# Where a two-layer decoder kernel computes the next layer's modulation: eight steps moved from the gate part to the output stage

## The chip, the cores and the metric

One Trainium2 chip, one core. The metric is the device time of one launch in microseconds, as the median of three runs. The engines are TensorE (PE, with its weight loads as PEld), VectorE (DVE), ScalarE (ACT), GpSimd (POOL) and SyncE (SP), which here only issues transfers.

## What is computed

Two layers over 256 tokens of 1024 channels. Each layer has a token mixer (retention and windowed attention) and a product-key retrieval over 128 x 128 single-neuron experts, and each is preceded by a normalization whose shift, scale and output gate depend on a condition vector:

```python
cond = jax.nn.silu(c)
for l in range(DEPTH):
    mod = cond @ ada_w[l] + ada_b[l]
    sh1, sc1, g1, sh2, sc2, g2 = jnp.split(mod, 6, axis=-1)
    h = rmsnorm(x, norm1_g[l]) * (1.0 + sc1[:, None]) + sh1[:, None]
    x = x + g1[:, None] * token_mixer(h, positions, w_in[l], ret_gn_g[l], sinks[l], w_out[l])
    h = rmsnorm(x, norm2_g[l]) * (1.0 + sc2[:, None]) + sh2[:, None]
    x = x + g2[:, None] * peer(h, peer_wq[l], peer_k1[l], peer_k2[l], peer_u[l], peer_v[l])
return rmsnorm(x, final_g)
```

`peer` picks 16 experts per head and token and computes `gelu(h . u[e]) * gate` for them, then the sum of these times `v[e]`. The kernel computes it densely for 224 of the 256 tokens: all `h . u` products, a matrix of gates that is zero for experts not picked, and all products with `v`. For the other 32 tokens it fetches the picked rows of `u` and `v`.

## The kernel before, in words

**Weight blocks.** All weights pass through the same pipeline in blocks of 128 x 1024 (512 KB). SP loads a block into one of four slots `raw` (L379), ScalarE rounds it into `w_hi` (`round_hi`, L552), VectorE makes the rest `w_lo = raw - w_hi` (`low`, L848), and TensorE multiplies with both. `w_hi` and `w_lo` have two slots each. A load waits until `low` of the block four earlier is done. Per layer there are 52 input blocks, 8 and 16 of two projections, 128 expert blocks `u` (numbered 0 to 127 here, the variable `m`) and 128 output blocks `v`. In the positions of the table below an output block has the number 128 (`N_U`) plus its own.

**The gate part.** The last 52 expert blocks, 76 to 127, run beside the building of the gate matrix in 28 batches of eight tokens. Batch b belongs to block `gate_after(b) = 76 + b * 50 // 28`: blocks 76, 77, 79, 81, 83, 84, 86, 88, 90, 92, 93, 95, 97, 99, 101, 102, 104, 106 and so on to 124, so that the distance is two blocks, and one block six times. In the block before its own, VectorE, ScalarE and GpSimd write the batch's one-hot operands (`hot`: on VectorE L1206 and L1210), then TensorE runs 16 small products behind the expert block (`gate`, L1703), which wait for all three. Beside them VectorE multiplies the activations with an earlier batch's gates (`weigh`, L1226, waits for the products of that batch) and with the next activation (`product`, L1233). TensorE's product of batch b also waits until batch b-2 is weighed.

**The output stage.** While TensorE works on output block m, ScalarE rounds a row block of the activations for block m+1 (`round_p`, L780) and VectorE makes its low rest (`low_p`, L1238) and the low rest of the weights (`low`). Then TensorE multiplies with `v`: first L1731, which begins only after `low_p`, then L1727, which waits for `low`. Beside this VectorE works for the 32 tokens: for 32 of the blocks 2 to 59 a dot product with a fetched row of `u` (`dot`, L1260, at block 2 + 57j//31), and for 32 of the blocks 61 to 118 a weighted addition of a fetched row of `v` (`mix`, L1277, at block 61 + 57j//31). GpSimd issues the fetch of the rows (L540).

**The modulation.** A modulation step is one `mod_block` (L852): VectorE multiplies a loaded block `ada` (128 x 1024) with the condition and sums along the row (L855). Every second one (odd number) also adds the bias to the last two sums (L859) and VectorE waits for that to be done. The steps are laid beside other work by tables of positions. `MOD_V_AT[l]` lists those of the expert and output blocks: `mod_beside(at)` is called once in each block, in the expert part right behind `low`, in the output stage behind `low_p` and `low` and ahead of `dot` and `mix`. SP loads step k's block (L391, two slots) right behind the weight block that stands five after the position of step k-2, if step k-2 is done. In layer 0 there are 18 such steps, numbers 46 to 63: the last two of layer 0's output gate, then shift and scale of layer 1's first normalization. In layer 1 there are two, at output blocks 4 and 10.

VectorE's order in an output block:

```python
if not (end and j == RING - 1):
    low_p(RING * i + j + 1, (j + 1) % 2)
if not (end and j == RING - 1 and l == DEPTH - 1):
    low(n0 + RING * i + j + 1, (j + 1) % RING)
mod_beside(N_U + RING * i + j)
for k in range(SP_STEPS):
    if dot_at(k) == RING * i + j:
        dot(k)
    if mix_at(k) == RING * i + j:
        mix(k)
```

Of the kernel before, what the change touches and what calls it, by code (L numbers as in the profile page):

```python
# [55 lines left out]
N_WOUT, N_WQ, N_U, N_V = KC, 2 * PH, NKEYS, NKEYS  # L56
# [16 lines left out]
          B_WQ + 1, B_WQ + 2, B_WQ + 3, B_WQ + 4, B_WQ + 5, B_WQ + 6)  # L73
PE_GROUP = 2
MOD_WIN = len(MOD_AT)
MOD_V_AT = (tuple(range(78, 78 + 3 * 16, 3)) + (N_U + 4, N_U + 10), (N_U + 4, N_U + 10))
MOD_L = (MOD_FIRST, MOD_FIRST + MOD_WIN + len(MOD_V_AT[0]))
assert MOD_L[1] + MOD_WIN + len(MOD_V_AT[1]) == DEPTH * N_MOD
V_COPIES = 5
# [143 lines left out]
def build(nc, x, c, positions, consts, decay, mask, vectors, ada, win, wout, wq, keys, u, v, u_rows, out):  # L223
    ctx = ExitStack()
    with ctx:
# [148 lines left out]
        def _(sp):  # L374
# [13 lines left out]
            def mod_load_v(n):  # L388

                sp.wait_ge(mod_used, n - 1)  # L390
                sp.dma_start(mod_ring2[:, n % 2, :], ada_all[n]).then_inc(mod_in2[n % 2], 16)  # L391
# [44 lines left out]
            for l in range(DEPTH):  # L436
                base = l * N_BLOCKS
                for q, (count, src) in enumerate(srcs):
# [39 lines left out]
                    def mods_beside(at):  # L478
                        for k in range(len(MOD_V_AT[l])):
                            if at == (MOD_V_AT[l][k - 2] + 5 if k > 1 else 4 * SPREAD_AT):  # L480
                                mod_load_v(MOD_L[l] + MOD_WIN + k)
# [358 lines left out]
        def _(dve):  # L840
# [119 lines left out]
            for l in range(DEPTH):  # L960
# [318 lines left out]
                def mod_beside(at):  # L1279

                    if at in MOD_V_AT[l]:
                        k = MOD_V_AT[l].index(at)
                        dve.wait_ge(mod_in2[k % 2], 16 * (len(MOD_V_AT[0]) // 2 * l + k // 2 + 1))
# [600 lines left out]
```

## Time and profile before

| | |
|---|---|
| three runs | 2009.29, 2010.58, 2012.95 us; median 2010.58 |
| profiled execution | 2010.33 us, its span from first to last instruction 2008.5 us |
| busy, share of the span | PE 97%, PEld 94%, DVE 85%, ACT 60%, POOL 22% |
| granted TensorE clock | 0.992 of full speed over the span |
| DMA | 480.55 MB, mean 239 GB/s |

The span is what the engines' timeline shows; the execution's own time is a little longer, by what lies around it. Shares are means over stages that have different limits, so the sections below read single stretches: the gate part of layer 0 is at about 515 to 686 us of the span, its output stage from 689 us on, and the same two stages of layer 1 start at about 1502 and 1671 us.

### The profile page before, as it was taken

Reading aid. Unit: us, or ns where it says so; the run is one execution under the profiler, and the core shown is the slowest. Engines: PE = TensorE matmul, PEld = TensorE weight load, DVE = VectorE, ACT = ScalarE, POOL = GpSimd, SP = SyncE. Lnnn points to the kernel's source line nnn. Section 1 sums busy time; section 2 is a strip of 40 time slices with the busy share of each in tenths; the row PEclk is TensorE's granted clock in tenths of the full one; section 3 lists DMA queues with packets and bytes.
Section 4 is the critical chain, followed back from the end, with each engine's and each line's share of the span. In section 5 each row is a group of like instructions: output and inputs, shape, how many; then the busy total and the mean of one; then the engine's idle time right before and its main releaser. Section 6 shows DMA issues by size and latency. Waiting matters only on the chain.

```text
span 2008.5 us, 41124 instructions
## 1 busy us (share of the span) xinstructions
PE 1956.6 (97%) x15412; PEld 1881.8 (94%) x15412; DVE 1712.2 (85%) x3168; ACT 1208.9 (60%) x2257; POOL 442.5 (22%) x300
## 2 busy tenths in 40 slices
PE   6999999999999999999989999999999999999998
PEld 6899899999999999999978898999999999999998
DVE  7876888999899888888777878899988888888887
ACT  3478545555888655555545775455568885555554
POOL 0000000000556434444100000000016553443440
PEclk8999999999999999999999999999999999999999
DMA  8764755666666799998767657656665558989984
GB/s 342 267 238 148 263 187 170 199 198 193 217 214 209 252 318 319 327 321 321 259 222 246 203 169 252 200 184 194 198 212 172 161 162 288 324 317 324 321 324 137
DMA packets 133555, 480.55 MB, mean 239 GB/s; under 512 B 16048, under 2 KB 16688, under 8 KB 132784
## 3 DMA queue, kind: packets, MB, share of 16 engines
q1 hardware_dynamic: 114992, 411.74, 61.5%
q0 software_dynamic: 18432, 67.12, 8.6%
q8 instruction: 76, 1.25, 0.3%
q14 instruction: 55, 0.45, 0.1%
HBM read 473.61 MB, written 1.57 MB: 237 GB/s over the span
## 4 chain that ended last, share of the span: by engine, by line
PE 86%; DVE 6%; ACT 3%; issue 2%; DMA 2%; SPq 1%; DVEq 0%; ACTq 0%
PE ps L1731 20%; PE ps L1397 14%; PE ps L1393 14%; PE ps L1394 13%; PE ps L1727 12%; PE ps L1476 2%; PE ps L1390 2%; PE ps L1703 2%; DVE w_lo L848 2%; ACT w_hi L552 1%; DMA raw<-in_win 1%; DVE hot L855 1%; PE ps L1664 1%; PE ps L1457 1%; PE ps L1565 1%
## 5 line engine op out<-in xcount | busy, mean ns | idle before, releaser
L552 ACT CAST w_hi<-raw 128x1024 fp32r<-128x1024 f32 x664 | 695.3, 1047 | 432.8 <-PE ps L1397 360.2
L848 DVE TENSOR_TENSOR w_lo<-raw,w_hi 128x1024 fp32r<-128x1024 f32 x664 | 811.1, 1222 | 167.4 <-ACT w_hi L552 163.4
L1393 PE MATMUL ps<-h_both,w_hi 128*128 128x224 f32 (+1 forms) x2680 | 633.1, 279 | 3.0 <-ACT big L557 1.5
L1394 PE MATMUL ps<-h_both,w_hi 128*128 128x224 f32 (+1 forms) x2680 | 624.9, 276 | 0.0
L1393 PEld LDWEIGHTS ps<-h_both,w_hi 128*128 128x128 f32 x2680 | 513.8, 192 | 6.2 <-issue 3.5
L1394 PEld LDWEIGHTS ps<-h_both,w_hi 128*128 128x128 f32 x2680 | 514.2, 192 | 0.0
L529 POOL TENSOR_SCALAR hot<-con,rt 128x128 f32<-128x128 f32 x168 | 198.9, 1194 | 1152.3 <-DVE neg L1313 1041.0
L1731 PE MATMUL ps<-p_both,w_hi 128*128 128x448 f32 x1952 | 440.1, 367 | 1.0 <-DVE p_both L1238 1.0
L1397 PE MATMUL ps<-h_both,w_lo 128*128 128x224 f32 (+1 forms) x2912 | 391.3, 277 | 0.4 <-DVE w_lo L848 0.4
L1731 PEld LDWEIGHTS ps<-p_both,w_hi 128*128 128x128 f32 x1952 | 349.3, 189 | 24.5 <-issue 1.3
L1397 PEld LDWEIGHTS ps<-h_both,w_lo 128*128 128x128 f32 x2912 | 362.2, 192 | 3.4 <-DVE w_lo L848 1.0
L780 ACT CAST p_both<-big 128x224 fp32r (+1 forms) x256 | 97.1, 380 | 303.5 <-PE ps L1727 301.1
L1727 PEld LDWEIGHTS ps<-p_both,w_lo 128*128 128x128 f32 x2048 | 269.2, 191 | 7.6
L1727 PE MATMUL ps<-p_both,w_lo 128*128 128x224 f32 x2048 | 272.8, 273 | 0.0
L540 POOL DMA_INDIRECT hot<-in_v,spare x64 | 123.6, 1931 | 174.3 <-DVE big L1277 144.6
L540 POOL DMA_INDIRECT hot<-in_u_rows,spare x64 | 119.8, 1872 | 185.5 <-DVE spare L1260 163.8
L1238 DVE TENSOR_TENSOR p_both<-big,p_both 128x224 fp32r<-128x224 f32 x256 | 99.5, 389 | 31.2 <-ACT p_both L780 29.9
L774 ACT ACTIVATE hot<-hot,rt,neg 128x128 f32<-128x128 f32 x224 | 92.5, 484 | 1.9
L855 DVE CUSTOM_DVE_ANT_0 hot<-hot,cond 128x1024 f32<-128x1024 f32 x60 | 73.2, 1220 | 9.4 <-DMA hot<-in_ada 9.4
L1277 DVE SCALAR_TENSOR_TENSOR big<-hot,spare,big 128x1024 f32<-128x1024 f32 x62 | 79.3, 1278 | 0.0
L1260 DVE CUSTOM_DVE_ANT_0 hot<-hot,big 128x1024 f32<-128x1024 f32 x64 | 78.0, 1219 | 0.0
L1226 DVE TENSOR_TENSOR big<-big,ps 128x1024 f32<-128x1024 f32 x56 | 68.4, 1221 | 7.5 <-PE ps L1703 0.5
(205 smaller groups left out, 1872.9 us busy)
## 6 DMA issues: line engine op xcount, KB each, us to landing
raw<-in_u SPq DMA_DIRECT2D x256, 512.0 KB
raw<-in_v SPq DMA_DIRECT2D x256, 512.0 KB
raw<-in_win SPq DMA_DIRECT2D x104, 512.0 KB
hot<-in_ada SPq DMA_DIRECT2D x60, 512.0 KB, 4.8
big<-in_ada SPq DMA_DIRECT2D x36, 512.0 KB, 5.6
raw<-in_wq SPq DMA_DIRECT2D x32, 512.0 KB
raw<-in_wout SPq DMA_DIRECT2D x16, 512.0 KB
big<-in_decay SPq DMA_DIRECT2D x2, 1536.0 KB, 12.4
```

What stands on the lines that cost most here:

```text
L529: last = nc.gpsimd.tensor_scalar(hot2[:, s, t, :], iota, rt[:, 1, col], rt[:, 2, col], ALU.is_equal, ALU.mult)
L540: nc.gpsimd.indirect_dma_start(rows_in[j % SP_SLOTS], None, u_flat if j < SP_STEPS else v_flat, bass.IndirectOffsetOnAxis(spread[:, 0, k:k ...
L552: nc.scalar.copy(w_hi[:, j % 2, :], raw[:, j, :]).then_inc(hi_ready, 1)
L780: nc.scalar.copy(p_hi[:, s, 0:nd], acts[:, ds(m, 1), 0:nd].rearrange("p a t -> p (a t)")).then_inc(phi_ready, 1)
L848: tt(w_lo[:, j % 2, :], raw[:, j, :], w_hi[:, j % 2, :].bitcast(F32), ALU.subtract).then_inc(lo_ready, 1)
L855: nc.vector.tensor_tensor_reduce(row, row, cond[:], 1.0, 0.0, ALU.mult, ALU.add, mod_sum[:, s:s + 1]).then_inc(mod_used, 1)
L1238: tt(p_lo[:, s, 0:nd], acts[:, ds(m, 1), 0:nd].rearrange("p a t -> p (a t)"), p_hi[:, s, 0:nd].bitcast(F32), ALU.subtract).then_inc(plo_re ...
L1393: mm(o, w, h_hi[:, k, 0:nd], start=(k == 0), stop=False)
L1394: mm(o, w, h_lo[:, k, 0:nd], start=False, stop=False)
L1397: last = mm(o, w_lo[:, s, P * k:P * (k + 1)], h_hi[:, k, 0:nd], start=False, stop=(k == KC - 1), skip_group_check=both)
L1727: return mm(bank(YC[c])[:, 0:nd], vv[:, s, P * c:P * (c + 1)], pp[:, s, 0:nd], start=False, stop=False, skip_group_check=True)
L1731: return mm(bank(YC[c])[:, 0:2 * nd].rearrange("p (a t) -> p a t", a=2), w_hi[:, s, P * c:P * (c + 1)], p_both[:, s, :, 0:nd], start=begin ...
```

## The change

Only the table `MOD_V_AT` of layer 0 is changed:

```diff
-MOD_V_AT = (tuple(range(78, 78 + 3 * 16, 3)) + (N_U + 4, N_U + 10), (N_U + 4, N_U + 10))
+MOD_V_AT = (tuple(range(78, 78 + 6 * 8, 6)) + tuple(range(N_U + 4, N_U + 4 + 11 * 10, 11)), (N_U + 4, N_U + 10))
```

Before, sixteen steps stand at expert blocks 78, 81, 84, ..., 123 and two at output blocks 4 and 10. Now eight stand at expert blocks 78, 84, 90, ..., 120 and ten at output blocks 4, 15, 26, 37, 48, 59, 70, 81, 92 and 103. The steps keep their order and numbers, so the one at block 84 is now an odd one and was an even one. The loads move along: eight of them from behind expert blocks to behind output blocks. Layer 1's table is the same. On TensorE, ScalarE and GpSimd nothing moves.

VectorE in the gate part of layer 0, from the one-hot operands of the batch of block 93 on to the first of block 95's, before (L1206 writes a batch's first operand, L1226 weighs a batch, L855 and L859 are the modulation step of block 93):

```order
L1206 TENSOR_TENSOR hot<-row,iota 128x1024
L1210 TENSOR_SCALAR hot<-con,rt 128x128
L848 TENSOR_TENSOR w_lo<-raw,w_hi 128x1024
L855 ISA big,mod_sum<-big,cond 128x1024
L855 ISA mod_sum 128x1
L859 TENSOR_TENSOR mod<-mod_sum,vec 128x2
L1233 TENSOR_TENSOR big<-big,acted 128x224
L1226 TENSOR_TENSOR big<-big,ps 128x128x8
L848 TENSOR_TENSOR w_lo<-raw,w_hi 128x1024
L1233 TENSOR_TENSOR big<-big,acted 128x224
L1226 TENSOR_TENSOR big<-big,ps 128x128x8
L1206 TENSOR_TENSOR hot<-row,iota 128x1024
```

The same place now:

```order
L1206 TENSOR_TENSOR hot<-row,iota 128x1024
L1210 TENSOR_SCALAR hot<-con,rt 128x128
L848 TENSOR_TENSOR w_lo<-raw,w_hi 128x1024
L1233 TENSOR_TENSOR big<-big,acted 128x224
L1226 TENSOR_TENSOR big<-big,ps 128x128x8
L848 TENSOR_TENSOR w_lo<-raw,w_hi 128x1024
L1233 TENSOR_TENSOR big<-big,acted 128x224
L1226 TENSOR_TENSOR big<-big,ps 128x128x8
L1206 TENSOR_TENSOR hot<-row,iota 128x1024
L1210 TENSOR_SCALAR hot<-con,rt 128x128
```

The modulation step of block 93 (three rows) has gone from between L848 and L1233; all else there is as it was.

VectorE in the output stage of layer 0, block 69, 70 and 71, before:

```order
L1238 TENSOR_TENSOR p_both<-big,p_both 128x224
L848 TENSOR_TENSOR w_lo<-raw,w_hi 128x1024
L1238 TENSOR_TENSOR p_both<-big,p_both 128x224
L848 TENSOR_TENSOR w_lo<-raw,w_hi 128x1024
L1277 SCALAR_TENSOR_TENSOR big<-hot,spare,big 128x1024
L1238 TENSOR_TENSOR p_both<-big,p_both 128x224
L848 TENSOR_TENSOR w_lo<-raw,w_hi 128x1024
```

The same place now:

```order
L1238 TENSOR_TENSOR p_both<-big,p_both 128x224
L848 TENSOR_TENSOR w_lo<-raw,w_hi 128x1024
L1238 TENSOR_TENSOR p_both<-big,p_both 128x224
L848 TENSOR_TENSOR w_lo<-raw,w_hi 128x1024
L855 ISA big,mod_sum<-big,cond 128x1024
L855 ISA mod_sum 128x1
L1277 SCALAR_TENSOR_TENSOR big<-hot,spare,big 128x1024
L1238 TENSOR_TENSOR p_both<-big,p_both 128x224
L848 TENSOR_TENSOR w_lo<-raw,w_hi 128x1024
```

The step of block 70 stands between that block's L848 and its `mix`; the L1238 issued in block 71, which is the `low_p` for block 72, comes behind both.

## Rows read from the trace of the kernel before

**Rows 1.** Busy time by window: gate part of layer 0, of layer 1, output stage of layer 0
```profile
core 0: us, PE busy (x) PEld busy (x) DVE busy (x) ACT busy (x) POOL busy (x), PEclk, DMA share, GB/s
510.00:690.00 180.00, 174.17 (x1747) 172.25 (x1747) 161.09 (x235) 147.56 (x336) 112.56 (x88) 1.00 0.69 223
1500.00:1670.00 170.00, 169.65 (x1718) 168.45 (x1718) 139.07 (x189) 145.33 (x332) 96.28 (x88) 1.00 0.56 180
690.00:988.00 298.00, 298.00 (x1891) 283.05 (x1890) 255.48 (x339) 157.06 (x237) 116.73 (x60) 1.00 0.90 316
```

**Rows 2.** Timeline of TensorE, gate products of layer 0: start, length, engine, line, count, idle
```profile
517.51 1.09 PE L1703 MATMUL ps<-hot 128*128 128x128 f16 x16
521.17 1.09 PE L1703 MATMUL ps<-hot 128*128 128x128 f16 x16
529.13 1.08 PE L1703 MATMUL ps<-hot 128*128 128x128 f16 x16 [1.43 <-DVE hot L1206]
...
545.46 1.09 PE L1703 MATMUL ps<-hot 128*128 128x128 f16 x16
552.84 1.08 PE L1703 MATMUL ps<-hot 128*128 128x128 f16 x16 [0.88 <-DVE hot L1206]
559.51 1.08 PE L1703 MATMUL ps<-hot 128*128 128x128 f16 x16 [0.20 <-issue]
...
575.84 1.09 PE L1703 MATMUL ps<-hot 128*128 128x128 f16 x16
583.70 1.08 PE L1703 MATMUL ps<-hot 128*128 128x128 f16 x16 [1.37 <-DVE hot L1206]
...
679.15 1.08 PE L1703 MATMUL ps<-hot 128*128 128x128 f16 x16 [0.26 <-issue]
```

**Rows 3.** The same view, gate products of layer 1
```profile
1505.20 1.09 PE L1703 MATMUL ps<-hot 128*128 128x128 f16 x16
...
1561.52 1.09 PE L1703 MATMUL ps<-hot 128*128 128x128 f16 x16
1567.86 1.09 PE L1703 MATMUL ps<-hot 128*128 128x128 f16 x16
...
1661.26 1.09 PE L1703 MATMUL ps<-hot 128*128 128x128 f16 x16
```

**Rows 4.** Timeline of VectorE, output stage of layer 0: its two modulation steps
```profile
701.87 1.22 DVE L855 CUSTOM_DVE_ANT_0 big<-big,cond 128x1024 f32<-128x1024 f32 x1
...
703.01 0.39 DVE L1238 TENSOR_TENSOR p_both<-big,p_both 128x224 fp32r<-128x224 f32 x1
...
716.94 1.21 DVE L855 CUSTOM_DVE_ANT_0 big<-big,cond 128x1024 f32<-128x1024 f32 x1
...
718.20 0.16 DVE L859 TENSOR_TENSOR mod<-mod_sum,vec 128x2 f32<-128x2 f32 x1
718.39 0.39 DVE L1238 TENSOR_TENSOR p_both<-big,p_both 128x224 fp32r<-128x224 f32 x1
```

**Rows 5.** Timelines of VectorE and TensorE, where the output stage begins
```profile
688.25 0.39 DVE L1238 TENSOR_TENSOR p_both<-big,p_both 128x224 fp32r<-128x224 f32 x1
688.79 0.44 PE L1731 MATMUL ps<-p_both,w_hi 128*128 128x448 f32 x1 [0.47 <-DVE p_both L1238]
```

**Rows 6.** The same views at output blocks 59 to 61 and 70 to 72
```profile
841.67 0.39 DVE L1238 TENSOR_TENSOR p_both<-big,p_both 128x224 fp32r<-128x224 f32 x1
842.77 1.80 PE L1731 MATMUL ps<-p_both,w_hi 128*128 128x448 f32 x8
...
869.48 0.39 DVE L1238 TENSOR_TENSOR p_both<-big,p_both 128x224 fp32r<-128x224 f32 x1
870.53 1.80 PE L1731 MATMUL ps<-p_both,w_hi 128*128 128x448 f32 x8
```

**Rows 7.** The page, DMA issues: KB each, median us from issue to landing
```profile
big<-in_ada SPq DMA_DIRECT2D x36, 512.0 KB, 5.6
```

## The prediction

> **What bounds the kernel now.** I read the windows first, for the two stages that the change touches, with the same stages of layer 1 beside them. TensorE is busy for 174.2 of 180 us in the gate part of layer 0, for 169.7 of 170 us in that of layer 1, and for all 298 us in the output stage [rows 1]. So TensorE's own work sets the pace nearly everywhere, at full clock, and an engine beside it costs time only where it makes TensorE wait. VectorE is close behind: 161 of 180 us in the first window, 255 of 298 us in the third.
>
> Then the starts of the gate products on TensorE. Undisturbed, two batches that lie two blocks apart start 6.34 us apart [rows 3]. From the first batch to the last, layer 1 takes 156.06 us and layer 0 takes 161.64 us [rows 2, 3]. The work is the same except for the sixteen modulation steps, so these cost 5.6 us now, and this is all that can be had in the gate part.
>
> Against 6.34 us behind the batch ahead, batches of layer 0 are late, each time behind a modulation step [rows 2]: that of block 79 by 1.62 us (529.13 - 521.17 - 6.34), of 86 by 1.04 (552.84 after 545.46), of 88 by 0.33, of 95 by 1.52 (583.70 after 575.84) and of 124, the last, by 0.41 behind that of 122. Block 104 repeats 86 (1.16), 106 repeats 88 (0.34), and 115 is late by 0.18. That is 6.6 us in eight places. The rest is free: VectorE does a step in otherwise idle time. A large one comes where the operands of two batches in succession have just been written (83 and 84, 92 and 93, 101 and 102) and the step stands ahead of the next two weighings.
>
> The third thing to see is a step's length on VectorE: 1.14 us from its start to the next operation for an even step, 1.45 us for an odd one, whose bias addition must be over first [rows 4].
>
> **What the change does in the gate part.** I go through the eight places.
> - 79: its step at block 78 stays, as does all before it. 1.62 us stay.
> - 86: the step at 84 stays, but becomes an odd one. Block 95 is the same place in the rhythm with an odd step and cost 1.52 us, so I take 1.52 instead of 1.04: 0.48 more.
> - 88 and 106: the steps at 87 and 105 go, and 0.33 + 0.34 with them.
> - 95: the step at 93 goes, and 1.52 with it.
> - 97: the step at 96 stays, becomes odd and stands in the block in which the next batch's operands are due, as those at 87 and 105 did. They cost 0.33 and 0.34. It cost nothing so far, because the stall at 95 had let ScalarE and VectorE catch up; without this I take 0.4, with 0.3 and 0.6 as ends.
> - 104 and 115: the steps stay and stay even: 1.16 and 0.18, unchanged.
> - 122: the step at 120 becomes odd, with the next operands one block later. I take 0.3, with 0 and 0.5 as ends (0.5 is what the odd form adds at block 86).
> - 124: the step at 123 goes: 0.41.
>
> The steps at 90 and 108 cost nothing before and have more room now. Gone: 0.33 + 0.34 + 1.52 + 0.41 = 2.6. New: 0.48 + 0.4 + 0.3 = 1.2. The gate part gets 1.4 us shorter. The eight steps that leave are 8 x 1.3 = 10 us of VectorE's time, but most of it stood in time that VectorE had over. What is late next is the same as now: the batches behind 78, 84 and 102.
>
> **What it does in the output stage.** An output block takes TensorE 2.52 us (from 842.77 to 870.53 us are eleven blocks [rows 6]). TensorE needs the low part of the activations (L1238) at the start of the block; it starts 0.15 us behind that operation's end [rows 5], which lasts 0.39 us, so the operation must start 0.54 us ahead of TensorE's block.
> - Steps at 4, 15, 26, 37 and 48 stand in blocks without a fetched row, but behind two and ahead of one that have one. VectorE then needs 2.58 us per block and cannot catch up for four blocks. The two steps of before show this: at block 4 (even) and at block 10 (odd) TensorE never waited. At 15 and 37 an odd step meets such a run of four, and by the same count the slack at its end is about 0.1 us. I cost all five at 0, with 0.2 us for each of the two as the upper end.
> - Steps at 59, 70, 81, 92 and 103 stand in a block that also has a dot product or a weighted addition, and are queued ahead of it. The next `low_p` comes behind both. At block 59 it started at 841.67 for a block that began at 842.77 [rows 6]. An odd step puts it to 843.12, and TensorE could start at 843.66: 0.89 us late. At block 70 it started at 869.48 for 870.53; an even step makes it 870.62 + 0.54 = 871.16: 0.63 us late. Block 92 (even) is as 70, and blocks 81 and 103 (odd) are as 70 with 0.31 us more: 0.94 each.
>
> The sum over the five blocks is 0.89 + 0.63 + 0.94 + 0.63 + 0.94 = 4.0 us. `low` is delayed too, but is needed 1.6 us into a block that itself starts late. The block behind is a free one or begins late itself, so nothing adds up. Nobody waits for the modulation itself: the last step is at block 103, the next layer needs it after block 127.
>
> In rows 4 the odd step's addition starts 0.12 us behind the point at which an even step's next operation does, and it and the wait for it take 0.19 us more, though it is 0.16 us long. The Trainium skill (VectorE: DVE Perf Modes, section "The DRAIN you can't avoid") says that a semaphore wait between two operations of VectorE adds nothing to what they take anyway. By that rule an odd step would be longer by its 0.16 us alone, half of what the rows give, and the three odd ones in mixed blocks would cost 0.45 us less. The sum goes by the rows.
>
> The loads: eight transfers of 512 KB move into the output stage. The DMA engines are busy there for 0.90 of the time at 316 GB/s [rows 1]. Eight blocks are 4.2 MB more on 94 MB, which brings the share to 0.94. A weight block's load is released by the end of `low` four blocks earlier, about 1.5 us behind 841.67 and so 0.4 us into block 61, and the weight is rounded early in the third block behind: 3 x 2.52 us less 0.4, and some 0.5 us for where in that block, make 7.7 us. A modulation block lands in 5.6 us [rows 7]; one queued ahead delays a weight by its transfer, 0.52 MB at 316 GB/s = 1.7 us. 5.6 + 1.7 is below 7.7, so I cost the loads at 0. Their steps come six blocks or more after them. Were this cover gone, each could cost up to 1.7 us. In the gate part the load was not the limit at a share of 0.69.
>
> **Sum.** -1.4 + 4.0 = 2.6 us, with ends from the bounds above: -1.8 to -1.0 in the gate part; 3.3 (if TensorE's start does not need the 0.15 us) to 4.4 in the output stage; together 1.5 to 3.4. The profiled execution took 2010.33 us, which makes 2013.0; it lies 0.25 us below the median of the runs, 2010.58, on which I put the forecast: **2013.2 us**. A measurement here can tell about 0.2% (4.0 us) from no change, so this counts as no change, barely on the slower side.
>
> **The rivals.**
> - *The output stage absorbs all.* For it: VectorE is idle for 43 of 298 us there, and two steps went unnoticed. Against: these two stood in blocks without a row. It would give -1.4, 2009.2 us. Chance 0.08.
> - *The gate part follows the density of steps rather than their places,* and falls half or all of the way to layer 1's: -2.8 to -5.6, with 4.0 in the output stage +1.2 to -1.6, so 2009 to 2012 us. For it: 5.6 us for sixteen steps is a mean of 0.35. Against: ten of the sixteen cost nothing, and the dearest places keep theirs. Chance 0.14.
> - *Both*: -5.6, 2005 us, **faster**. Chance 0.05.
> - *The weights come late in the output stage*, **slower**. Mechanism: SP's queue is in order, so each modulation block stands ahead of three weight loads, while GpSimd's row fetches fill the DMA engines to 0.90. It decides where the landing exceeds 7.7 us minus 1.7 = 6.0 us; the median is 5.6, so it is near. Then each of the eight loads costs TensorE 0.5 to 1.7 us: 4 to 14 us on top, 2017 to 2027 us. The Trainium skill (DMA: Bandwidth & Descriptors, section "Queues, rings and completion order") has each DMA engine alternate between the queues that have work, packet by packet; by that a modulation block ahead of a weight could cost twice its own transfer while rows are fetched, which no row here shows. Chance 0.11.
> - *The change doing less than it says* is excluded: all eighteen steps are still there on VectorE, at the blocks that the table names.
>
> **How the numbers follow.** The forecast has 0.62. Of that, 0.09 may show as more than 4.0 us, since the median comes from three runs and those of before spread over 3.7 us. Slower is then 0.11 + 0.09 = 0.20, faster is 0.05, and the rest, 0.75, is within 0.2%. The range takes in the forecast's ends, the density case and the start of the DMA case, with about 1 us for the spread of the runs: 2009.5 to 2017.
>
> **What would show it.** Right: in the gate part of layer 0 the batches of 79, 86 and 104 late by 1.6, 1.5 and 1.2 us, those of 88, 95, 106 and 124 on time, 97 and 122 slightly late; from first to last batch 160.2 us. In the output stage five blocks of TensorE (61, 72, 83, 94, 105) that start 0.6 to 0.9 us late, released by L1238, and none at 15 to 48. Wrong: those five on time, stalls at 17, 18, 39 or 40, or ScalarE's L552 waiting for `raw` in the output stage.

## The result, and the profile after

| | before | after |
|---|---|---|
| median of 18 runs each, side by side | 2010.78 us | 2014.06 us |
| lowest, highest | 2007.77, 2014.62 us | 2011.73, 2017.59 us |
| ratio | | 1.0018, 95% interval 1.0012 to 1.0024 |
| span of the profiled execution | 2008.5 us | 2012.4 us |

The change costs 0.18% by the ratio, which is 3.6 us, with 2.4 and 4.8 us as the ends of the interval. The two profiled spans differ by 3.9 us.

The two windows of layer 0, in the view and with the columns of [rows 1]:

```profile
core 0: us, PE busy (x) PEld busy (x) DVE busy (x) ACT busy (x) POOL busy (x), PEclk, DMA share, GB/s
510.00:690.00 180.00, 175.16 (x1756) 173.09 (x1756) 151.41 (x214) 148.32 (x336) 105.58 (x88) 1.00 0.62 200
690.00:988.00 298.00, 294.95 (x1861) 279.29 (x1860) 260.66 (x354) 154.87 (x234) 110.27 (x60) 1.00 0.91 327
```

VectorE was relieved in the gate part (161.1 to 151.4 us busy) and got 5 us more in the output stage (255.5 to 260.7). TensorE, which was busy for all of the 298 us there, now lacks 3 us of them. The DMA share went from 0.90 to 0.91 and the rate from 316 to 327 GB/s.

The gate products of layer 0 in the changed kernel, the view of [rows 2]:

```profile
518.74 1.09 PE L1703 MATMUL ps<-hot 128*128 128x128 f16 x16
522.80 1.08 PE L1703 MATMUL ps<-hot 128*128 128x128 f16 x16
530.92 1.08 PE L1703 MATMUL ps<-hot 128*128 128x128 f16 x16 [1.46 <-DVE hot L1206]
...
547.25 1.09 PE L1703 MATMUL ps<-hot 128*128 128x128 f16 x16
555.15 1.08 PE L1703 MATMUL ps<-hot 128*128 128x128 f16 x16 [1.41 <-DVE hot L1206]
561.48 1.09 PE L1703 MATMUL ps<-hot 128*128 128x128 f16 x16
...
577.82 1.09 PE L1703 MATMUL ps<-hot 128*128 128x128 f16 x16
584.16 1.09 PE L1703 MATMUL ps<-hot 128*128 128x128 f16 x16
591.12 1.08 PE L1703 MATMUL ps<-hot 128*128 128x128 f16 x16 [0.47 <-DVE hot L1206]
...
607.45 1.09 PE L1703 MATMUL ps<-hot 128*128 128x128 f16 x16
614.83 1.08 PE L1703 MATMUL ps<-hot 128*128 128x128 f16 x16 [0.88 <-DVE hot L1206]
...
679.57 1.09 PE L1703 MATMUL ps<-hot 128*128 128x128 f16 x16
```

From first to last they take 160.83 us, where it was 161.64. The batch of 86 (555.15) starts 7.90 us behind that of 84, 1.56 us more than the undisturbed 6.34 us. The batch of 88 (561.48) is now on time, and so is that of 95 (584.16, 6.34 us behind 577.82). The batch of 97 (591.12) is late by 0.62 us, 104 by 1.04 us. The second row is 4.06 us behind the first, where one block with a batch takes 3.66 us: 0.40 us that the kernel before did not show in its profiled execution.

All lateness in the gate part, and what the first to the last batch take (in us; worked out from each timeline in the same way; a dash is less than 0.05). The last row is layer 1 of the kernel before, which has no modulation step there:

| batch of block | 77 | 79 | 86 | 88 | 95 | 97 | 104 | 106 | 115 | 122 | 124 | first to last |
|---|---|---|---|---|---|---|---|---|---|---|---|---|
| before | - | 1.62 | 1.04 | 0.33 | 1.52 | - | 1.16 | 0.34 | 0.18 | - | 0.41 | 161.64 |
| after | 0.40 | 1.78 | 1.56 | - | - | 0.62 | 1.04 | - | 0.19 | 0.22 | - | 160.83 |
| before, layer 1 | 0.15 | 0.59 | 0.24 | - | - | - | - | - | - | - | - | 156.06 |

So not all lateness in layer 0 comes from the steps: 0.98 us of it is there without any. This is why 6.6 us of lateness before make only 5.6 us more than layer 1.

The output stage, VectorE and TensorE of the changed kernel where its step at block 59 stands and at block 72, the view of [rows 6]:

```profile
841.21 1.22 DVE L855 CUSTOM_DVE_ANT_0 big<-big,cond 128x1024 f32<-128x1024 f32 x1
842.47 0.16 DVE L859 TENSOR_TENSOR mod<-mod_sum,vec 128x2 f32<-128x2 f32 x1
842.67 1.22 DVE L1260 CUSTOM_DVE_ANT_0 hot<-hot,big 128x1024 f32<-128x1024 f32 x1
843.82 0.39 DVE L1238 TENSOR_TENSOR p_both<-big,p_both 128x224 fp32r<-128x224 f32 x1
844.26 1.90 PE L1731 MATMUL ps<-p_both,w_hi 128*128 128x448 f32 x8 [0.64 <-DVE p_both L1238]
...
846.88 1.80 PE L1731 MATMUL ps<-p_both,w_hi 128*128 128x448 f32 x8
...
872.64 1.90 PE L1731 MATMUL ps<-p_both,w_hi 128*128 128x448 f32 x8 [0.37 <-DVE p_both L1238]
```

The modulation step (L855 at 841.21, L859) and the dot product (842.67) stand in a row, the `low_p` for block 61 comes at 843.82, and TensorE starts at 844.26, 0.64 us of it idle with `low_p` as the releaser. Block 61 begins 3.33 us behind block 60, not 2.52. It then takes 2.62 us itself, up to the start of block 62 at 846.88, which is 0.10 us more than usual: its eight L1731 take 1.90 us, those of the next block 1.80. Five blocks of the stage are like this, and TensorE's waits in it, summed (columns: who waited for whom, us in total, times, longest), are:

```profile
PE ps L1731 <- DVE p_both L1238: 3.0, 5, 1.0
```

The idle time in this view is shorter than the lateness, since an undisturbed block starts 0.17 us before the last matmuls of the one ahead of it end. By the starts, the blocks are late by 0.81, 0.53, 0.86, 0.54 and 1.14 us (blocks 61, 72, 83, 94, 105), and each then takes 0.10 longer itself. That is 4.37 us. Three more, 28 to 30, are late by 0.10, 0.07 and 0.06 us. Together 4.6 us, and the stage is 4.58 us longer by the starts of its blocks. -0.81 + 4.58 = 3.8 us. That the spans differ by nearly the same, 3.9 us, is partly luck: in these two executions the part ahead of the first gate product took 1.2 us longer (518.74 against 517.51), and all that follows the output stage took 1.1 us less.

### The profile page after: what moved, and what is told of

The parts are those of the page before. It is cut to its first block, busy times and chain, and to the rows that moved or that the text cites. A ratio compares the mean times of both kernels' runs of the same rounds, so it can differ in the third digit from the quotient of the medians.

```text
span 2012.4 us, 41126 instructions
## 1 busy us (share of the span) xinstructions
PE 1958.5 (97%) x15412; PEld 1883.7 (94%) x15412; DVE 1711.8 (85%) x3168; ACT 1208.4 (60%) x2257; POOL 427.4 (21%) x300
## 4 chain that ended last, share of the span: by engine, by line
PE 86%; DVE 7%; ACT 3%; issue 2%; DMA 1%; SPq 0%; ACTq 0%; DVEq 0%
PE ps L1731 19%; PE ps L1397 15%; PE ps L1393 14%; PE ps L1394 13%; PE ps L1727 12%; PE ps L1703 2%; PE ps L1476 2%; PE ps L1390 2%; DVE w_lo L848 2%; ACT w_hi L552 2%; PE ps L1631 1%; DMA raw<-in_win 1%; PE ps L1664 1%; PE ps L1457 1%; DVE hot L855 1%
## 5 line engine op out<-in xcount | busy, mean ns | idle before, releaser
L848 DVE TENSOR_TENSOR w_lo<-raw,w_hi 128x1024 fp32r<-128x1024 f32 x664 | 811.0, 1222 | 173.4 <-ACT w_hi L552 169.7
L1731 PE MATMUL ps<-p_both,w_hi 128*128 128x448 f32 x1952 | 440.9, 368 | 4.0 <-DVE p_both L1238 4.0
L529 POOL TENSOR_SCALAR hot<-con,rt 128x128 f32<-128x128 f32 x168 | 190.3, 1143 | 1160.6 <-DVE neg L1313 1041.8
L1731 PEld LDWEIGHTS ps<-p_both,w_hi 128*128 128x128 f32 x1952 | 349.3, 189 | 28.4 <-DVE p_both L1238 4.0
L540 POOL DMA_INDIRECT hot<-in_v,spare x64 | 119.3, 1864 | 182.9 <-DVE big L1277 152.7
L1238 DVE TENSOR_TENSOR p_both<-big,p_both 128x224 fp32r<-128x224 f32 x256 | 99.4, 388 | 29.3 <-ACT p_both L780 28.2
L855 DVE CUSTOM_DVE_ANT_0 hot<-hot,cond 128x1024 f32<-128x1024 f32 x60 | 73.2, 1220 | 8.5 <-DMA hot<-in_ada 8.2
L1226 DVE TENSOR_TENSOR big<-big,ps 128x1024 f32<-128x1024 f32 x56 | 68.4, 1221 | 7.2
```

Source lines behind the costliest of these rows:

```text
L529: last = nc.gpsimd.tensor_scalar(hot2[:, s, t, :], iota, rt[:, 1, col], rt[:, 2, col], ALU.is_equal, ALU.mult)
L540: nc.gpsimd.indirect_dma_start(rows_in[j % SP_SLOTS], None, u_flat if j < SP_STEPS else v_flat, bass.IndirectOffsetOnAxis(spread[:, 0, k:k ...
L848: tt(w_lo[:, j % 2, :], raw[:, j, :], w_hi[:, j % 2, :].bitcast(F32), ALU.subtract).then_inc(lo_ready, 1)
L855: nc.vector.tensor_tensor_reduce(row, row, cond[:], 1.0, 0.0, ALU.mult, ALU.add, mod_sum[:, s:s + 1]).then_inc(mod_used, 1)
L1238: tt(p_lo[:, s, 0:nd], acts[:, ds(m, 1), 0:nd].rearrange("p a t -> p (a t)"), p_hi[:, s, 0:nd].bitcast(F32), ALU.subtract).then_inc(plo_re ...
L1731: return mm(bank(YC[c])[:, 0:2 * nd].rearrange("p (a t) -> p a t", a=2), w_hi[:, s, P * c:P * (c + 1)], p_both[:, s, :, 0:nd], start=begin ...
```

## The experiments

The place theory: a modulation step costs what it puts in front of an operation that TensorE waits for, and nothing anywhere else. Its rivals: VectorE's load decides (the number of steps in a stage, the density theory), or the eight moved transfers do (the load theory). Each kernel below was measured against the kernel before on the same chip. All compute the same thing; only the table, or one call, differs.

**Free blocks.** The change's gate part, but the steps of the output stage in blocks without a fetched row.

```diff
-MOD_V_AT = (tuple(range(78, 78 + 6 * 8, 6)) + tuple(range(N_U + 4, N_U + 4 + 11 * 10, 11)), (N_U + 4, N_U + 10))
+MOD_V_AT = (tuple(range(78, 78 + 6 * 8, 6)) + tuple(N_U + b for b in (4, 19, 30, 41, 52, 65, 76, 87, 98, 109)), (N_U + 4, N_U + 10))
```

> The change's eight steps in the gate part are kept; the ten of the output stage stand at blocks 4, 19, 30, 41, 52, 65, 76, 87, 98 and 109, none of which has a fetched row, and none is next to two such blocks in succession. Place theory (a step costs where the next low_p comes behind both it and a row): the five late blocks go, the output stage runs at 2.52 us per block throughout, the gate part stays as in the change (about 0.8 us shorter than before), so the time is 0.8 to 1.4 us below the kernel before, 4 to 5 us below the change. Density theory (the ten steps load VectorE by the same amount wherever they stand): the 4 to 5 us stay. Load theory (the eight more transfers make weights late): they stay too, as waits of ScalarE for raw.

Measured: 2008.42 us, ratio to before 0.9989 (0.9980 to 0.9998), 2.2 us faster (0.4 to 4.0) and, by the two ratios, 5.8 us below the change; the profiled spans of these two differ by 4.4 us. The window of the output stage, columns as above:

```profile
690.00:988.00 298.00, 298.00 (x1892) 283.03 (x1891) 263.54 (x358) 157.43 (x237) 117.02 (x60) 1.00 0.92 330
```

TensorE is busy for all of it again, though VectorE has more to do (263.5 us) than in the change (260.7) and the DMA rate is as high. From the first block on, the stage takes 307.28 us where it took 307.17 before and 311.75 in the change, and no block is late by more than 0.10 us. The density and the load theory both said that the loss would stay. They fall for this stage. The gate part is the change's, but took 161.51 us and so only 0.13 us less than before, since batch 77 is late by 1.22 us here; the last experiment comes to this.

**Two mixed blocks.** The converse: the kernel before, with only its two steps of the output stage moved into blocks that have a row.

```diff
-MOD_V_AT = (tuple(range(78, 78 + 3 * 16, 3)) + (N_U + 4, N_U + 10), (N_U + 4, N_U + 10))
+MOD_V_AT = (tuple(range(78, 78 + 3 * 16, 3)) + (N_U + 59, N_U + 70), (N_U + 4, N_U + 10))
```

> The kernel before with its two steps of the output stage moved from blocks 4 and 10 to 59 (even) and 70 (odd), both of which have a fetched row; the gate part is untouched. Place theory: block 61 starts 0.6 to 0.7 us late and block 72 0.9 to 1.0, with 0.1 us more each in the block behind, so 1.6 to 1.8 us slower than before. Density theory: the number of steps and loads is the same, so no change, within 0.3 us.

Measured: 2011.67 us, ratio 1.0007 (0.9998 to 1.0017), which is 1.4 us, on the edge of what can be told from nothing. The trace tells it: TensorE's waits in the output stage are

```profile
PE ps L1731 <- DVE p_both L1238: 1.0, 2, 0.7
```

and none in the kernel before. Block 61 starts 0.48 us late (0.6 to 0.7 expected), block 72 0.86 (0.9 to 1.0), and each takes 0.10 longer itself: 1.54 us in all, and the stage takes 308.69 us, 1.52 more than before. The same number of steps and loads, at two other places, makes the loss.

**Gate gaps.** The free-blocks kernel, with the eight steps of the gate part where VectorE has nothing due.

```diff
-MOD_V_AT = (tuple(range(78, 78 + 6 * 8, 6)) + tuple(N_U + b for b in (4, 19, 30, 41, 52, 65, 76, 87, 98, 109)), (N_U + 4, N_U + 10))
+MOD_V_AT = ((81, 83, 90, 92, 99, 101, 108, 117) + tuple(N_U + b for b in (4, 19, 30, 41, 52, 65, 76, 87, 98, 109)), (N_U + 4, N_U + 10))
```

> Output stage as in the free-blocks run; the eight steps of the gate part at 81, 83, 90, 92, 99, 101, 108 and 117: either the first of two successive gate blocks (behind which VectorE idles 1.65 us in layer 1 until ScalarE has rounded) or two ahead of it. Place theory: no gate product is late, the gate part takes layer 1's 156.1 us instead of 161.6, so 5 to 6 us below before and 4 to 5 us below the free-blocks run. Density theory: eight steps are eight steps, no difference from the free-blocks run within 0.5 us.

Measured: 2004.51 us, ratio 0.9968 (0.9957 to 0.9980), 6.4 us below before and some 4 us below the free-blocks kernel. Its first to last gate product take 156.56 us (free blocks: 161.51; layer 1 before: 156.06), and only the batches of 77 (0.91) and 79 (0.57) are late. I had expected none, but 79 is late by 0.59 us in layer 1 too, where no step stands. Eight steps stand in the gate part as in the change, and they cost nothing that the traces show. Why, is seen on VectorE in layer 1 of the kernel before, where the weights' low part is made in block 93:

```profile
1560.93 1.28 DVE L848 TENSOR_TENSOR w_lo<-raw,w_hi 128x1024 fp32r<-128x1024 f32 x1 [1.66 <-ACT w_hi L552]
```

It has been idle for 1.66 us until ScalarE, busy with the operands of two batches in succession, has rounded these weights. A step at block 92 falls into this idle time; the one at 93 of the kernel before stood behind it. So the number of steps was not what cost time there either.

**All in the output stage.** No step in the gate part, eighteen in free blocks of the output stage.

```diff
-MOD_V_AT = (tuple(range(78, 78 + 3 * 16, 3)) + (N_U + 4, N_U + 10), (N_U + 4, N_U + 10))
+MOD_V_AT = (tuple(N_U + b for b in (4, 10, 17, 23, 28, 34, 39, 45, 50, 56, 65, 71, 76, 82, 87, 93, 98, 104)), (N_U + 4, N_U + 10))
```

> No step in the gate part; all eighteen of layer 0 in free blocks of the output stage (4, 10, 17, 23, 28, 34, 39, 45, 50, 56, 65, 71, 76, 82, 87, 93, 98, 104), with sixteen transfers more there than before. Place theory: gate part as in layer 1, output stage undisturbed: 5 to 6 us below before, as the gate-gaps run. Load theory: the DMA share of the output stage reaches 0.97 or more, ScalarE waits for raw several times, and it is slower than the gate-gaps run by 1 us or more. Density theory: the output stage loses more than in the change, 5 us or more, so no faster than before.

Measured: 2005.17 us, ratio 0.9972 (0.9961 to 0.9983), 5.6 us below before. The output stage now has sixteen transfers more than before:

```profile
690.00:988.00 298.00, 298.00 (x1893) 283.12 (x1892) 272.64 (x378) 157.34 (x237) 117.91 (x60) 1.00 0.94 341
```

The DMA share is 0.94 at 341 GB/s, not the 0.97 that I had put down, and ScalarE waits for a weight once, for 0.2 us. TensorE is never idle, and VectorE is busy for 272.6 of 298 us. The stage takes 307.50 us. The steps at 71, 82, 93 and 104 stand directly ahead of two blocks in succession with a row, and each of these pairs makes one block 0.08 to 0.09 us late: this is the price of a step ahead of such a pair (all four steps are odd ones), where the prediction had said that slack would be about 0.1 us. The measurement does not separate this kernel from the gate-gaps kernel.

**Parity.** The kernel before without the step at 81 and with one more at output block 17. All later gate steps keep their place and change between even and odd.

```diff
-MOD_V_AT = (tuple(range(78, 78 + 3 * 16, 3)) + (N_U + 4, N_U + 10), (N_U + 4, N_U + 10))
+MOD_V_AT = ((78,) + tuple(range(84, 126, 3)) + (N_U + 4, N_U + 10, N_U + 17), (N_U + 4, N_U + 10))
```

> The kernel before without its step at block 81, and one more in the output stage at the free block 17: so every later step of the gate part keeps its place and changes between even and odd. If the bias addition of an odd step and the wait for it are what made block 86 dearer in the change, the lateness swaps: batch 86 about 1.5 us (even before: 1.04), 95 about 1.05 (odd before: 1.52), 104 about 1.5 (even before: 1.16), 88 and 106 on time (odd before: 0.33), 124 about 0 (odd before: 0.41). If the place alone decides, all stay within 0.15 us of before. The sum of both is nearly the same, so the time is that of before within 0.7 us either way.

A single run each, 2012.71 us beside 2010.39 us for before. Both lie within what the kernel before took in its 18 runs, so the times say nothing about the 0.7 us that I had expected at most; the trace does. The gate products of 84, 86, 93 and 95:

```profile
545.64 1.09 PE L1703 MATMUL ps<-hot 128*128 128x128 f16 x16
553.46 1.08 PE L1703 MATMUL ps<-hot 128*128 128x128 f16 x16 [1.32 <-DVE hot L1206]
...
576.13 1.09 PE L1703 MATMUL ps<-hot 128*128 128x128 f16 x16
583.66 1.08 PE L1703 MATMUL ps<-hot 128*128 128x128 f16 x16 [1.04 <-DVE hot L1206]
```

The batch of 86 is late by 1.48 us (7.82 - 6.34; before 1.04), that of 95 by 1.19 (before 1.52), 104 by 1.49 (before 1.16), 88 and 106 are on time (before 0.33 and 0.34), 124 is late by 0.09 (before 0.41). The lateness swapped at all six places. Two were not in my expectation: 97 is late by 0.31 and 115 by 0.62, since their steps (96 and 114) became odd too. First to last batch take 161.86 us, 0.22 more than before. So the form decides along with the place: where a batch is due, an odd step costs 0.3 to 0.4 us more than an even one. At 97 the odd step makes the batch late even behind the stall of 95, where the even one had not.

**Row first.** The change, with the modulation step called behind the row's operation.

```diff
-                        mod_beside(N_U + RING * i + j)
                         for k in range(SP_STEPS):
                             if dot_at(k) == RING * i + j:
                                 dot(k)
                             if mix_at(k) == RING * i + j:
                                 mix(k)
+                        mod_beside(N_U + RING * i + j)
```

> The change with the modulation step called behind the dot product or weighted addition of its output block instead of ahead of it. If what matters is that the next low_p comes behind both, blocks 61, 72, 83, 94 and 105 stay late by the same amounts within 0.15 us each; only ScalarE's wait for the last dot product (1.4 us) goes. If the row operation is what is waited for (by ScalarE at block 60, by GpSimd's fetches), the lateness shrinks by half or more, to 2 us or less in sum.

A single run, 2012.31 us. TensorE's waits in the output stage:

```profile
PE ps L1731 <- DVE p_both L1238: 2.8, 5, 0.7
```

Still five. The blocks are late by 0.80, 0.54, 0.85, 0.54 and 0.85 us, the same as in the change within 0.02 us except for the last (1.14 there). ScalarE's wait for the last dot product is gone and has changed nothing. So at four of the five places it is the sum of the two operations ahead of `low_p` that counts, and not which of them comes first; the fifth moved by 0.29 us, more than the 0.15 us that I had allowed. The last block's surplus in the change is visible in its trace of VectorE:

```profile
956.60 0.16 DVE L859 TENSOR_TENSOR mod<-mod_sum,vec 128x2 f32<-128x2 f32 x1
957.07 1.29 DVE L1277 SCALAR_TENSOR_TENSOR big<-hot,spare,big 128x1024 f32<-128x1024 f32 x1 [0.32 <-DVE mod L859]
958.27 0.39 DVE L1238 TENSOR_TENSOR p_both<-big,p_both 128x224 fp32r<-128x224 f32 x1
```

The operation behind the bias addition starts 0.47 us behind the start of that addition, where it was 0.19 us at block 10 of the kernel before [rows 4] and 0.20 at block 59 above. That is 0.28 us more, the whole surplus. Why it took longer here, no run shows.

**Late loads.** The lateness of batch 77 differs from execution to execution: 0.40 us in the change, 1.22, 0.58, 0.91 and 0.27 in the first four experiments in their order, none in the kernel before, in parity and in row first. In each of these five ScalarE waits for a weight there, by 0.6, 1.4, 0.8, 1.1 and 0.4 us. The first two modulation loads are issued behind block 76's, ahead of the following weights, in both layers of all these kernels. This kernel has steps only at places that had cost nothing, and issues these two loads later.

```diff
-MOD_V_AT = ((81, 83, 90, 92, 99, 101, 108, 117) + tuple(N_U + b for b in (4, 19, 30, 41, 52, 65, 76, 87, 98, 109)), (N_U + 4, N_U + 10))
+MOD_V_AT = ((90, 92, 99, 101, 108, 117) + tuple(N_U + b for b in (4, 10, 19, 28, 34, 41, 52, 65, 76, 87, 98, 109)),
+            (N_U + 4, N_U + 10))
...
-                            if at == (MOD_V_AT[l][k - 2] + 5 if k > 1 else 4 * SPREAD_AT):
+                            if at == (MOD_V_AT[l][k - 2] + 5 if k > 1 else 4 * SPREAD_AT + 4 + 3 * k):
```

> Steps only at places that cost nothing in the gate-gaps and all-output runs: six in the gate part (90, 92, 99, 101, 108, 117), twelve in free blocks of the output stage, and the first two modulation loads moved from behind expert block 76 to behind 80 and 83. If those two loads, which stand ahead of the weights of the first gate blocks in SP's queue, are what makes batch 77 late by 0.3 to 1.2 us in five of the runs (ScalarE waits for raw there), it is on time or within layer 1's 0.15 us, ScalarE has no DMA wait at 76 to 79, and the time is 0.3 to 1.2 us below the gate-gaps kernel on the same chip. If the lateness has another cause, it stays and the two are equal within 0.3 us.

> The gate-gaps kernel once more, as the mate of the late-loads run on the same chip: 5 to 6.5 us below before, batch 77 late by 0.3 to 1.2 us.

Measured on one chip: late loads 2003.26 us, ratio 0.9966 (0.9954 to 0.9978); gate gaps again 2003.41 us, ratio 0.9966 (0.9952 to 0.9979). The rounding of the weights around the first batches, and SP's issues, in the gate-gaps kernel (its first profiled execution):

```profile
506.53 0.59 SPq L379 DMA_DIRECT2D raw<-in_u  x1
507.16 1.84 SPq L391 DMA_DIRECT2D big<-in_ada  x2
509.38 9.55 SPq L379 DMA_DIRECT2D raw<-in_u  x5
511.04 1.06 ACT L552 CAST w_hi<-raw 128x1024 fp32r<-128x1024 f32 x1 [2.03 <-PE ps L1397]
516.28 1.05 ACT L552 CAST w_hi<-raw 128x1024 fp32r<-128x1024 f32 x1 [1.07 <-DMA raw<-in_u]
```

and in the late-loads kernel:

```profile
508.71 7.23 SPq L379 DMA_DIRECT2D raw<-in_u  x5
515.99 0.43 SPq L391 DMA_DIRECT2D big<-in_ada  x1
513.22 1.05 ACT L552 CAST w_hi<-raw 128x1024 fp32r<-128x1024 f32 x1 [2.02 <-PE ps L1397]
517.28 1.04 ACT L552 CAST w_hi<-raw 128x1024 fp32r<-128x1024 f32 x1
```

In the first, ScalarE waits 1.07 us for block 77's weight, which was issued behind two modulation blocks (L391 at 507.16), 2.85 us behind block 76's (509.38 against 506.53). In the second it was issued 0.63 us behind block 76's, the wait is gone, batch 77 is on time, 79 is late by 0.29 us, and first to last batch take 155.37 us, against 156.56 and 156.05 in the two executions of gate gaps.

In the second of those, batch 77 is late by 0.17 us, less than the 0.3 that I had expected at least. ScalarE's wait there, 2.3 us, is not of this kind: it is for block 76's weight, which is issued ahead of the two modulation blocks, and only some 0.2 us of it come on top of its usual wait for TensorE at this place (2.03 and 2.02 in the rows above). The late-loads kernel has the same wait for block 76 in layer 1, 2.3 us, with no modulation load near it.

So the traces show that the two loads hold up block 77's weight. That batch 77 stays on time without them rests on two cases, one in each layer of this kernel; with them it was on time in 6 of 18 (nine executions, two layers). A gain in time is not shown: the two medians differ by 0.15 us, and each ratio is only known to about 2.4 us either way.

## Why the prediction was right

The forecast was 2.6 us slower and no change by the 0.2% bound; measured are 3.6 us (2.4 to 4.8). The time lies in the range, and the mechanism was the forecast one: fewer late batches in the gate part, five late blocks in the output stage, released by `low_p`. The size was too small: the sum's own ends were 1.5 to 3.4 us, and the two stages make 3.8 us in the traces. With this the ratio (0.18%) stays only just below the bound of 0.2%, and the interval reaches past it (0.24%). By its steps:

- **Gate part, -1.4 us forecast, -0.8 measured.** 88, 95, 106 and 124 came on time as forecast. 86 has 1.56 (1.52 forecast), 104 1.04 (1.16), 115 0.19 (0.18), 122 0.22 (0.3). 97 has 0.62, the upper end of what I gave; the parity and free-blocks kernels repeat it (0.31 for an odd step behind a stall, 0.62 without one). The term that was missing is batch 77: I went through the places that were late in one execution, and this one is late in most others. 0.40 of the 0.6 us are there, and it belongs to the loads at block 76, not to the change. So it was wrong that the load was not the limit in the gate part. Without batch 77, the change's gate part takes 160.43, 160.29 and 160.46 us in its three executions (the change, free blocks, row first), that of before 161.64 and 161.58 in two (before, two mixed blocks): 1.2 us less, close to the forecast.
- **Readings of the gate part.** I put all eight late batches down to the steps. Layer 1 has 0.98 us of lateness with none, 0.59 of it at 79, so the step at block 78 costs about 1.0 of the 1.62 us (an estimate from these rows; 79 is late by 0.3 to 0.8 us in the four executions of kernels without that step). And if eight batches are late, eight of the sixteen steps cost nothing, not ten, as I wrote under the density rival. Neither enters the sum.
- **Five free blocks with a step, 0 forecast.** Blocks 4, 15, 37 and 48 cost nothing, the two odd ones among them. 0.23 us came at 28 to 30, behind the step at 26 and a wait of ScalarE for a weight just ahead of it (0.6 us), the only DMA wait of the stage. The row-first kernel has the same step at 26, no such wait there, and these blocks on time, so the step alone does not make them late.
- **Five mixed blocks, 4.0 us forecast, 4.4 measured.** 0.81, 0.53, 0.86, 0.54 and 1.14 us against 0.89, 0.63, 0.94, 0.63 and 0.94. The first four start about 0.1 us less late than forecast: TensorE began 0.05 us behind the end of `low_p` (843.82 + 0.39 to 844.26), not 0.15 us. The block itself then took 0.10 us longer, which gives back the same and was not in my sum. The rest is the long wait behind L859 in the last one. The two-mixed-blocks and free-blocks kernels show that the place makes this loss, and the row-first kernel that the order within the block does not.
- **The page's rule.** By the rule of the Trainium skill (VectorE: DVE Perf Modes, "The DRAIN you can't avoid") an odd step would have been only 0.16 us longer than an even one. The same place with either kind gives 0.33 us: block 61 is late by 0.81 us with an odd step (the change) and 0.48 with an even one (two mixed blocks), block 72 by 0.86 and 0.53. The rows were the better price. The page's test was made with copies. Here the addition reads what the step's accumulator read has just written, and starts 0.12 us later than the next operation behind an even step, which has the same accumulator read [rows 4]; what happens in the 0.12 us was not tried.
- **The loads, 0 forecast.** In the output stage true to 0.2 us, and even with eight more (0.2 us of waiting at a share of 0.94). The forecast share for the change, 0.94, was too high: 0.91 was measured.
- **The rivals.** The density of steps is refuted on both sides (gate gaps, free blocks); absorption by the output stage holds for free blocks only; late weights did not come in the output stage, but for the 0.2 us at 28 to 30.

The step that I had not drawn from my own count: if only the places cost, then better places exist. The gate-gaps kernel is 6.4 us (4.0 to 8.6) faster than before and beats both kernels; the late-loads kernel is its equal.

## What to carry to other kernels

An engine that is busy for 85% of a stage can take more work for nothing at one block and lose 0.9 us by it at the next, so ask for each place what the next operation in that queue is and how long before the need of its consumer it starts; here the slack was 0.6 us behind the work that was already in these blocks, and the moved step 1.14 to 1.45 us long. Extra work belongs directly ahead of a wait that the engine has anyway (1.66 us in the gate part), not behind it. A step with a dependent small operation behind it is dearer than its busy time says (0.33 us for an operation of 0.16), and a change in the table that shifts parity moves this price to other places.

## What the runs showed of the hardware

A block that TensorE began after waiting for `low_p` took 0.10 us longer itself than undisturbed ones, each time (12 cases in three kernels: 0.09 to 0.11 us). The same weight load, that of block 77 in layer 0, behind the same two transfers in one queue, made ScalarE wait between 0 and 1.4 us in nine executions of kernels that do not differ up to that point. The DMA engines gave 341 GB/s over 298 us of one output stage, and ScalarE waited once in it for a weight, for 0.2 us.
